# Four groups fewer ahead of the attention units, and a ratio of 13:3 for 25:6, in the two cross attentions

## The reference

```
def cross_attention(h, mem_n, wq, wkv, wo):        # h: 512 x 1024, mem_n: 256 x 1024
    q = (h @ wq).reshape(B, S, X_HEADS, X_HEAD_DIM)             # 4 heads of 256
    kv = (mem_n @ wkv).reshape(B, M, 2, X_HEADS, X_HEAD_DIM)
    s = jnp.einsum('bshd,bmhd->bhsm', q, kv[:, :, 0]) * X_HEAD_DIM ** -0.5
    p = jax.nn.softmax(s, axis=-1)
    o = jnp.einsum('bhsm,bmhd->bshd', p, kv[:, :, 1]).reshape(B, S, D_MODEL)
    return o @ wo
...
for l in range(DEPTH):                                          # DEPTH = 2
    h = h + (even_mixer or odd_mixer)(rms_norm(h, norm_mix_g[l]), ...)
    h = h + cross_attention(rms_norm(h, norm_xattn_g[l]), mem_n, xattn_wq[l], xattn_wkv[l], xattn_wo[l])
    h = h + sq_relu_mlp(rms_norm(h, norm_mlp_g[l]), mlp_w1[l], mlp_w2[l])
return rms_norm(h, final_norm_g)
```

## Time and profile before

| | us |
|---|---|
| median of three runs | 2255.74 (2253.75 to 2256.54) |
| the profiled execution | 2253.75 |
| its span, first to last instruction | 2252.0 |
| TensorE busy in it | 2213.1 (98%) |
| DVE busy | 1464.2 (65%) |
| ACT busy | 979.4 (43%) |
| mean granted TensorE clock | 0.994 of full speed |

### The profile page before, as it was taken

How to read it: one execution, slowest core, us unless ns; L and a number is a source line. 1 busy time by engine, 2 the same in 40 slices (tenths; PEclk the granted TensorE clock), 3 DMA queues, 4 the chain that set the end, 5 groups by cost and what they waited for, 6 DMA issues and landing times.

```text
span 2252.0 us, 31942 instructions
## 1 busy us (share of the span) xinstructions
PE 2213.1 (98%) x12184; PEld 1860.6 (83%) x12184; DVE 1464.2 (65%) x2466; ACT 979.4 (43%) x1688; POOL 14.5 (1%) x14
## 2 busy tenths in 40 slices
PE   9999999999999999999999899999999999899998
PEld 7777778888777888888898789998888888799997
DVE  5866565557656556686665767766655657677775
ACT  5444543344445244364454544443323435344443
POOL 0000000000000000200000000000000000000000
PEclk9999999999999999999999999999999999899999
DMA  5655433245545323454353233332323213233331
GB/s 198 187 158 170 134 129 107 94 141 176 169 147 154 100 103 121 132 164 143 116 161 118 69 105 101 105 103 97 94 92 103 85 40 102 75 112 95 94 113 57
DMA packets 136696, 268.17 MB, mean 119 GB/s; under 512 B 21773, under 2 KB 79931, under 8 KB 136160
## 3 DMA queue, kind: packets, MB, share of 16 engines
q1 hardware_dynamic: 136544, 266.13, 37.3%
HBM read 235.37 MB, written 26.77 MB: 116 GB/s over the span
## 4 chain that ended last, share of the span: by engine, by line
PE 93%; DVE 3%; ACT 1%; issue 1%; DMA 1%; POOL 0%; SPq 0%; DVEq 0%; POOLq 0%; ACTq 0%
PE ps L2067 29%; PE ps L2069 29%; PE ps L2068 29%; PE ps L2084 2%; PE ps L2095 2%; ACT t_Tb L2291 1%; POOL t_UP L2050 0%; DVE t_wlo L2383 0%; PE ps L2119 0%; DVE t_UP L2643 0%; PE ps L2109 0%; PE ps L2107 0%; PE ps L2108 0%; PE ps L2121 0%; PE ps L2120 0%
## 5 line engine op out<-in xcount | busy, mean ns | idle before, releaser
L2067 PE MATMUL ps<-t_P0H,t_whi 128*128 128x512 f32 (+1 forms) x1560 | 587.0, 376 | 3.3 <-DVE t_P0L L2428 2.7
L2068 PE MATMUL ps<-t_P0L,t_whi 128*128 128x512 f32 (+1 forms) x1560 | 578.8, 371 | 0.0
L2069 PE MATMUL ps<-t_P0H,t_wlo 128*128 128x512 f32 (+1 forms) x1464 | 551.0, 376 | 0.0
L2067 PEld LDWEIGHTS ps<-t_P0H,t_whi 128*128 128x128 f32 x1560 | 293.9, 188 | 78.8 <-issue 23.6
L2210 ACT ACTIVATE t_whi<-t_raw 128x1024 fp32r<-128x1024 f32 (+2 forms) x287 | 292.3, 1023 | 151.9 <-PE ps L2069 150.3
L2383 DVE TENSOR_TENSOR t_wlo<-t_raw,t_whi 128x1024 fp32r<-128x1024 f32 (+2 forms) x284 | 335.8, 1184 | 33.8 <-PE ps L2069 25.6
L2068 PEld LDWEIGHTS ps<-t_P0L,t_whi 128*128 128x128 f32 x1560 | 293.8, 188 | 54.1 <-issue 1.0
L2069 PEld LDWEIGHTS ps<-t_P0H,t_wlo 128*128 128x128 f32 x1464 | 275.2, 188 | 54.0
L2067 PE MATMUL ps<-t_P1H,t_whi 128*128 128x512 f32 (+1 forms) x516 | 197.4, 382 | 2.1 <-DVE t_P1L L2768 1.0
L2068 PE MATMUL ps<-t_P1L,t_whi 128*128 128x512 f32 (+1 forms) x516 | 195.6, 379 | 0.0
L2069 PE MATMUL ps<-t_P1H,t_wlo 128*128 128x512 f32 (+1 forms) x500 | 191.7, 383 | 0.0
(11 more groups left out here) (341 smaller groups left out, 3923.6 us busy)
## 6 DMA issues: line engine op xcount, KB each, us to landing
t_raw<-in_wts SPq DMA_DIRECT2D x362, 512.0 KB, 3.5
far<-t_Tb SPq DMA_DIRECT2D x26, 384.0 KB, 2.9
far<-t_Tb SPq DMA_DIRECT2D x16, 512.0 KB, 3.1
t_PTX<-far SPq DMA_DIRECT2D x64, 96.0 KB, 3.0
t_raw<-in_wts SPq DMA_DIRECT2D x16, 384.0 KB, 3.0
t_QKV<-far SPq DMA_DIRECT2D x32, 128.0 KB, 3.4
t_raw<-in_wts SPq DMA_DIRECT2D x13, 256.0 KB, 2.9
t_PTX<-far SPq DMA_DIRECT2D x24, 128.0 KB, 3.7
```

Of the source, the lines that this page charges most:

```text
L2067: e.matmul(s.out, s.sh, s.mh, start=s.first, stop=False, skip_group_check=again)
L2068: e.matmul(s.out, s.sh, s.ml, start=False, stop=False, skip_group_check=again)
L2069: i = e.matmul(s.out, s.sl, s.mh, start=False, stop=s.end, skip_group_check=again)
```

## The change

The lead falls from six to two in both layers, and in layer 1 the ratio goes from 25/6 (4.17 steps at each place) to 13/3 (4.33). In layer 0 the ratio stays at 5.

```diff
@@ -1548,9 +1548,9 @@
                             yield
 
         if l == 0:
-            drive(main(), fill(), 5, 1, lead=6)
+            drive(main(), fill(), 5, 1, lead=2)
         else:
-            drive(main(), fill(), 25, 6, lead=6)
+            drive(main(), fill(), 13, 3, lead=2)
         if open_:
             open_.append(wo(2))
             for _ in range(6):
```

## The result

Four runs of the changed kernel take 2266.9 us (median, 2266.17 to 2269.02), four of the kernel before beside them 2256.14 (2253.75 to 2256.56): ratio 1.0051, 95% interval 1.0034 to 1.0068 (the ratio of the two medians alone is 1.0048). Three of these four runs of before are the ones on which the prediction stood, so this comparison has the prediction's own base in it. The prediction's own ratio was 2262.0 / 2255.74 = 1.0028. The profiled execution takes 2267.52, its span is 2265.7.

What follows compares the result with a forecast made beforehand. TensorE was taken to bound both stretches. Terms 3.33 (both S0) + 1.27 (S2) + 1.97 (S4) + 0.50 (V6) - 0.69 (D) = 6.4 us on a median of 2255.74 gave 2262 us, range 2257 to 2267.

Steps and rivals of the forecast that it cites:

- S6: Layer 1, head 3's query tile: no wait, 0.2 us to spare.
- handover at S: From the end of DVE's L2743 to TensorE's start at S: 0.04 us, taken from L2768 behind V5.
- base: Time of the kernel before that the sum was added to: 2255.74 us, the median of three runs.
- Rival 1: DVE and ACT catch up during S0's wait, so S2, S4 and V6 don't wait: +2.6 us, 2258.4; chance 0.17.
- S0: Start of both layers' stretches: TensorE waits for the second query tile, 1.68 us in layer 1, 1.65 in layer 0.
- V6: Layer 0, unit 6: TensorE waits for L2765 behind two weight splits, 0.39 us, 0.50 with the slow first matmul.
- S2: Layer 1: TensorE waits for head 1's second query tile, 1.16 us, 1.27 with the slow first matmul.
- S4: Layer 1: TensorE waits for head 2's query tile, 1.86 us, 1.97 with the slow first matmul.
- D: Layer 1, the wait behind V5 for L2768: one more group of matmuls fills it, -0.69 us.
- Rival 2: New waits drop TensorE's clock to 0.50, losing 2.5 us: 2264.6 at one wait, 2272 at all four; chance 0.10.
- Rival 3: Later timing spares the second MLP its clock drop of 2.5 us: +3.9 us, 2259.6; chance 0.11.

Runs made afterwards that it cites:

- e10: Kernel before with a lead of 5 instead of 6 in layer 1 alone and K's operands waited for ahead of the query tile at S: 2257.72 us, ratio 0.9997.
- second measurement: The changed kernel again, unaltered, five fresh runs against 21 of the kernel before: 2266.21 us against 2258.38, ratio 1.0039 (1.0026 to 1.0051).
- e7: Kernel before with a lead of 5 instead of 6 in both layers, ratios 5 and 25/6 kept: 2258.15 us, ratio 0.9999.
- e11: Changed kernel with TensorE waiting at S for K's parts first and the query tile (L2743) last: one execution, 2265.51 us.
- e8: Kernel before, unchanged, as a control: median 2257.79 us of 11 runs, ratio 0.9999.

## Why the prediction fell short

- **Places and mechanism of the waits: right.** All six terms are where they were forecast, with the operands waited for and the order in DVE's list that were forecast; S6 has no wait. Two steps failed, both in the sizes: the handover at S and the base. Rival 1 (only S0 waits) is refuted by the profile.
- **The failed term of the sum is the handover at S.** The forecast took 0.04 us from the end of L2743 to S, from L2768 and a group that waits for one semaphore. That row was read rightly (it is 0.05), but it isn't the price of an S, where two wait instructions follow; the trace of before has them at S0 too, at 1782.5 and 1782.6. Measured is 0.26 at all S, and 0.15 at V6. So S0 is 1.78 + 0.07 (slow first matmul, forecast 0.11) = 1.85 twice (forecast 3.33 for both), S2 1.37 + 0.08 = 1.45 (1.27), S4 2.09 + 0.08 = 2.17 (1.97), V6 of layer 0 0.51 + 0.07 = 0.58 (0.50), D -0.69 (-0.69). The sum is 7.2 instead of 6.4: this step is worth 0.8 us.
- **D: exact.** The wait ends 1.58 behind V5 where before it was 1.57, and e10 wins it without the rest.
- **The base was low, and this is the larger failure.** The sum was put on 2255.74, the median of three runs; 59 runs put the kernel before at about 2258.1. That is 2.4 of the 4 to 5 us by which 2262.0 is too low. It doesn't touch the ratio of the second measurement, but it does that of the first, whose runs of before include the same three. Against a base of 2258.1 the change costs 8.1 to 8.8 us, not the 10.8 of the first measurement.
- **Rival 2 came in part.** Behind the gap of 2.2 to 2.3 us at S4 the clock fell in two of six profiles that have it, for 1.5 us each (the rival had put 2.5 on it). Behind the gaps of 1.6 at S2 and 2.0 at S0 it never did. On average that is 0.5 us, for which the forecast had no term.
- **Rival 3 fell.** The MLPs' falls cost the changed kernel 6.0 and 8.1 us in two profiles and the kernel before 5.0, 5.2, 6.6 and 8.2 in four: nothing is spared.
- **What is left.** 2262.0 + 2.4 (base) + 0.8 (waits) + 0.5 (clock) = 2265.7, measured 2266.2 and 2266.9. The remaining 0.5 to 1.2 us can't be told from spread; since one fall more or less is already 1.5 us, it is in part luck that the remainder is so small. The changed kernel's three profiles lost 9.5 us to the clock on average and before's four 7.2, but before's alone reach from 4.95 to 10.52: whether the changed order brings more falls elsewhere stays open.

## What to carry to other kernels

A lead of fill ahead of a block is worth what the block's slowest operand is late, to be counted from DVE's and ACT's lists and not only from TensorE's; here six groups left 1.2 us of margin at S0, a lead of four already waits there and at one later block, a lead of two at two later ones, by a changed order of DVE's list. Put the wait for the operand that comes last behind the others, so that their wait instructions don't lie on the path; that was worth 0.11 us at each place that waits. A price taken from one handover holds only for another with as many wait instructions, so count them. And before a forecast is put on a few runs, ask whether they are typical: compare them with many, and take out of a profile what it lost to the clock.

## What the runs showed of the hardware

- From the end of a DVE instruction to TensorE's matmul are 0.05 us where no wait instruction of its own stands between (the first L2768 to L2067, in all profiles that have this wait), 0.15 where one does (L2765 to V6, L2383 to L2067 in e7, every S in e11), and 0.26 where two do (every S that waits in the other kernels, once 0.29). Each of them takes 51 ns in the trace and makes the distance 0.09 to 0.11 us longer. V6's, and that of L2067 in e7:

```profile
L2116 PEldq EVENT_SEMAPHORE  x1: 51/51/51, 1178.8 to 1178.8; - x1
L2065 PEldq EVENT_SEMAPHORE  x1: 51/51/51, 1173.1 to 1173.1; - x1
```
- Gaps of TensorE of the same length, with the same or much the same work around them, are followed by 0.50 in one execution and 1.00 in another: in the cross attentions at 2.2 to 2.3 us in two of six, at 2.49 in none of one, at 3.4 in one of two, at 4.05 in two of two; at 1.5 to 2.0 in none of 15. At 1021 us, where the gap holds eight matmuls of one column, 2.87 to 3.02 was followed by a fall in all of 12 profiles, and 2.53 and 2.71 in neither of two. The Trainium skill, TensorE: Matmul & The Clock Gate, section "Part 1: The HAM clock gate (the "warmup" mystery)", says that the gate's watch runs free of the kernel; by that rule equal gaps may end differently, and the runs agree.
- The gap at 1021 goes with a DMA: DVE's L2730 waits for t_E from hrow, 0.95 us in the first profile of before and 1.14 in e8 (gaps 2.53 and 2.71), 1.36 in e10 (2.94), 1.57 in the changed kernel and 1.94 and 1.89 in the two slower executions of before (3.02 each). From about 1.5 us on the gap no longer grows. So a transfer that lands 0.8 to 1 us later goes with 0.3 to 0.5 us of gap and, behind it, with a fall that costs 1.3 to 2.3 us. No run moved the transfer by itself, so the cause is argued here and not shown.
